# A single-core two-block transformer kernel: reordering its second attention stage and turning the sign of its logits

## What is computed

```
q, k normalised by head (RMS), B heads' last 32 dimensions rotated
logits = (q . k) * scale + bias or causal mask
p      = exp(logits - rowmax(logits));  p = p / rowsum(p)
out    = p . v
x      = x + concat(out_A, out_B) @ w_o
```

## Time and profile before

| what | value |
|---|---|
| median of 3 runs | 827.97 us (826.56 to 829.21) |
| the profiled execution | 827.33 us |
| its span in the trace | 825.5 us |
| PE busy | 813.6 us (99%) |
| DVE, ACT, POOL busy | 584.4, 464.6, 112.1 us |
| the stage of the change | from 565.8 us (`qk(0)`) to 642.5 us (first product of the last feed-forward part) |

### The profile page before, as it was taken

The page is one execution under the profiler, slowest core; times in us unless marked ns, Lnnn a source line. Parts: engine busy times, 40 slices in busy tenths (PEclk is TensorE's granted clock), DMA queues, the critical chain, the costliest instruction groups (busy, mean ns, idle before and its releaser), DMA issues.

```text
span 825.5 us, 15302 instructions
## 1 busy us (share of the span) xinstructions
PE 813.6 (99%) x6672; PEld 739.2 (90%) x6672; DVE 584.4 (71%) x745; ACT 464.6 (56%) x596; POOL 112.1 (14%) x76
## 2 busy tenths in 40 slices
PE   9999999999999999999999999998999999999998
PEld 7999988999999998888888799987888888888886
DVE  6968994985966587666666687688866875566653
ACT  6769775654443674544444574456676654444442
POOL 0102780660000000000000000000661000000000
PEclk9999999999999999999999999999999999999999
DMA  8845453443554655556555655554331555555541
GB/s 312 289 156 167 165 181 103 160 158 137 176 166 145 225 184 192 175 194 203 180 186 196 201 180 183 169 196 153 104 103 52 204 204 192 177 193 204 194 163 52
DMA packets 23827, 143.93 MB, mean 174 GB/s; under 512 B 2722, under 2 KB 4786, under 8 KB 7376
## 3 DMA queue, kind: packets, MB, share of 16 engines
q1 hardware_dynamic: 22576, 139.47, 49.4%
q0 software_dynamic: 1040, 3.43, 1.2%
q10 hardware_dynamic: 144, 0.04, 0.0%
HBM read 141.87 MB, written 1.06 MB: 173 GB/s over the span
## 4 chain that ended last, share of the span: by engine, by line
PE 91%; DVE 4%; ACT 3%; DMA 1%; issue 0%; SPq 0%; POOL 0%
PE ps L1773 11%; PE ps L1774 11%; PE ps L1775 11%; PE ps L2155 7%; PE ps L2148 7%; PE ps L2064 6%; PE ps L2062 6%; PE ps L2063 6%; PE ps L2153 4%; PE ps L2150 4%; PE ps L1839 1%; PE ps L1946 1%; PE ps L1842 1%; PE ps L1845 1%; DVE wlo L1004 1%; PE ps L1799 1%
## 5 line engine op out<-in xcount | busy, mean ns | idle before, releaser
L1004 DVE TENSOR_TENSOR wlo<-raw,whi 128x2048 fp32r<-128x2048 f32 x128 | 292.7, 2288 | 74.2 <-ACT whi L498 73.0
L498 ACT ACTIVATE whi<-raw 128x2048 fp32r<-128x2048 f32 x128 | 243.7, 1906 | 128.7 <-DMA raw<-w 128.5
L1773 PE MATMUL ps<-xx,whi 128*128 128x256 f32 x840 | 242.5, 289 | 0.0
L1774 PE MATMUL ps<-xx,whi 128*128 128x256 f32 x840 | 238.1, 283 | 0.0
L1775 PE MATMUL ps<-xx,wlo 128*128 128x256 f32 x840 | 238.0, 283 | 0.0
L1773 PEld LDWEIGHTS ps<-xx,whi 128*128 128x128 f32 x840 | 161.5, 192 | 1.8 <-issue 0.5
L1774 PEld LDWEIGHTS ps<-xx,whi 128*128 128x128 f32 x840 | 161.6, 192 | 0.2
L1775 PEld LDWEIGHTS ps<-xx,wlo 128*128 128x128 f32 x840 | 161.5, 192 | 0.0
L2062 PE MATMUL ps<-whi,xx 128*128 128x512 f32 x216 | 84.1, 390 | 0.0
L2063 PE MATMUL ps<-whi,xx 128*128 128x512 f32 x216 | 84.1, 389 | 0.0
L2064 PE MATMUL ps<-wlo,xx 128*128 128x512 f32 x216 | 84.0, 389 | 0.0
(11 more groups left out here) (295 smaller groups left out, 1125.0 us busy)
## 6 DMA issues: line engine op xcount, KB each, us to landing
raw<-w SPq DMA_DIRECT2D x128, 1024.0 KB, 4.9
raw<-w SPq DMA_DIRECT2D x8, 256.0 KB, 7.6
x<-xT SPq DMA_DIRECT2D x4, 256.0 KB, 5.5
raw<-w SPq DMA_DIRECT2D x2, 512.0 KB, 8.3
work<-bias_scratch POOLq DMA_DIRECT2D x1, 1024.0 KB, 6.9
out<-x SPq DMA_DIRECT2D x3, 256.0 KB, 2.4
work<-lnr POOLq DMA_DIRECT2D x1, 512.0 KB, 6.9
work<-sgw POOLq DMA_DIRECT2D x1, 512.0 KB, 7.6
```

Source lines behind the costliest of these rows:

```text
L498: A(hi, full, ACT.Copy).then_inc(sem("hi_ready"), 1)
L1004: V.tensor_tensor(lo, full, hi.bitcast(F32), ALU.subtract)\
L1773: mm(out, hi, xh[:, tile, :], start=start, stop=False, skip_group_check=skip)
L1774: mm(out, hi, xl[:, tile, :], start=False, stop=False, skip_group_check=skip)
```

## The change

All of it lies in the second attention stage and just ahead of it.

1. **Sign.** The A keys' gain and the B keys' gain are multiplied by -1, the bias is subtracted instead of added, and the mask is negated once (a new DVE instruction), so that `logits_row` makes minus the logits. Their row minimum is then directly the bias of `exp(-1 * l + min)`; L1479 falls away in all eight steps. `softmax_exp` waits for the two minima (steps 0 to 3) or for the four custom instructions (steps 4 to 7).
2. **PE's order.** The 48 blocks of `w_uq` go in six pieces of eight with a `qk` and `turn`, or a `pv`, between two pieces; `qk(1)` and `turn(0)` come behind the first piece instead of ahead of it. Groups go to banks 0, 1, 2, 0. The first two units of `w_o` are cut in smaller parts that are spread over steps 4 to 6, and the two units overlap. `rope_turned` comes ahead of all of these.
3. **DVE's order.** `rotary` goes ahead of the stage. `logits_row(p)` comes ahead of `queries_factor(p - 3)`; `keys_norm` goes from behind `heads_lo(1)` to behind `logits_row(2)`; the low part of the last `w_uq` unit a step earlier; the two `add_wo` of the first unit behind `logits_row(5)`.
4. **ACT's order.** The two sines go ahead of two squares; `softmax_exp(0)` ahead of `keys_copy(0)`; `rope_copy` and one `split_hi` ahead of `softmax_exp(1)`.

PE's order, as the diff has it:

```diff
-            qk(1)
-            turn(0)
-            for n in range(3):
...
-                for blk in range(16):
...
-                    if blk == 8:
-                        pv(n)
-                        if n == 0:
-                            rope_turned()
-                        if n == 2:
-                            keys_turned(0)
...
-                used(last)
-                if n:
-                    queries_stats(n - 1)
-                qk(2 + n)
-                turn(1 + n)
+            rope_turned()
+
+            def queries(first, end):
...
+                    if i == 0:
+                        pe.wait_ge(sem("evac0"), FILLS[U_UK][0])
+                    elif i % 12 == 0 and j < 3:
+                        pe.wait_ge(sem("uk_ev"), j)
+                    elif i % 12 == 0:
+                        pe.wait_ge(sem("uq_ev"), 1)
+                    last = mm3(ps[j % 3][:, (h % 2) * T:(h % 2 + 1) * T], u % SLOTS, blk * P, k, k == 0, k == 5)
...
+            queries(0, 8)
+            qk(1)
+            turn(0)
+            queries(8, 16)
+            pv(0)
+            queries(16, 24)
+            qk(2)
+            turn(1)
+            queries(24, 32)
+            pv(1)
+            queries(32, 40)
+            qk(3)
+            turn(2)
+            queries_stats(0)
+            queries(40, 48)
+            pv(2)
+            keys_turned(0)
+            pe.wait_ge(sem("uq_ev"), 3)
+            wo_part(0, 0, range(4), (1, 2))
+            wo_part(0, 1, range(4), (1, 2))
+            qk(4)
+            turn(3)
+            queries_stats(1)
+            wo_part(0, 2, range(4), (1, 2))
+            pv(3)
+            keys_turned(1)
+            pe.wait_ge(sem("uq_ev"), 4)
+            wo_part(1, 0, (0, 1), (0, 1))
+            wo_part(1, 1, (0, 1), (0, 1))
+            qk(5)
+            turn(4)
+            queries_stats(2)
+            used(wo_part(0, 3, range(4), (1, 2)))
+            wo_part(1, 2, (0, 1), (0, 1))
+            pv(4)
+            wo_part(1, 3, (0, 1), (0, 1))
+            pe.wait_ge(sem("wo_x"), 1)
+            for k in range(3):
+                wo_part(1, k, (2, 3), (0, 1))
+            used(wo_part(1, 3, (2, 3), (0, 1)))
+            qk(6)
+            turn(5)
+            queries_stats(3)
 
             pe.wait_ge(sem("wo_x"), 2)
-            wo_part(2, 0, (0, 1), (1, 2))
+            wo_part(2, 0, (0, 1), (2, 0))
             pv(5)
```

DVE's and ACT's programs, cut to what moves:

```diff
-                            ins = V.scalar_tensor_tensor(L[:, sl], ps[3 + hh][:, sl], rh[:, r:r + 1], tab[s], ALU.mult, ALU.add)
+                            ins = V.scalar_tensor_tensor(L[:, sl], ps[3 + hh][:, sl], rh[:, r:r + 1], tab[s], ALU.mult, ALU.subtract)
...
-                V.tensor_scalar(smx[:, p % 2, 1, :], smx[:, p % 2, 0, :], -1.0, None, ALU.mult).then_inc(sem("head_max"), 1)
+                    V.tensor_reduce(m4[:, :, 0], L2[:, :, 0:P], AX, ALU.min).then_inc(sem("head_max"), 1)
+                    V.tensor_reduce(m4[:, :, 1], L2[:, :, P:384], AX, ALU.min).then_inc(sem("head_max"), 1)
...
             logits_row(2)
-            ahead(U_UK)
+            keys_norm()
             normalise(2)
             heads_lo(1)
-            keys_norm()
-
+
+            logits_row(3)
             queries_factor(0)
-            logits_row(3)
             ahead(U_UQ)
...
+            logits_row(5)
+            queries_factor(2)
             dve.wait_ge(sem("unit_used"), U_WO + 1)
-            add_wo(0, 0)
-            add_wo(1, 1)
-            queries_factor(2)
-            logits_row(5)
+            add_wo(0, 1)
+            add_wo(1, 2)
             ahead(U_UQ + 2)
             normalise(5)
             heads_lo(4)
             ahead(U_WO)
 
+            logits_row(6)
             queries_factor(3)
-            logits_row(6)
...
+            softmax_exp(0)
             keys_copy(0)
-            softmax_exp(0)
             keys_copy(1)
+            rope_copy()
 
             probs_copy(0)
+            ahead(U_UK)
             softmax_exp(1)
             heads_hi(0)
-            rope_copy()
-            ahead(U_UK)
             queries_evac(0)
```

More of the change, by code:

```diff
@@ L820, in _ @@
             ahead(U_KR)
-            heads_sq(2)
-            ahead(U_KA)
-            heads_sq(3)
             act.wait_ge(sem("ang"), 1)
@@ L827, in _ @@
             A(cosk[64:96, 0, :], ang[64:96, 0, :], ACT.Sin).then_inc(sem("sin"), 1)
+            heads_sq(2)
+            ahead(U_KA)
+            heads_sq(3)
             ahead(U_KA + 1)
@@ L833, in softmax_exp @@
             def softmax_exp(p):
-                act.wait_ge(sem("head_max"), p + 1)
+                if p < 4:
+                    act.wait_ge(sem("head_max"), 2 * p + 2)
+                else:
+                    act.wait_ge(sem("head_l"), 4 * p + 4)
                 for hh in range(2):
@@ L1573, in _, with rotary @@
             V.tensor_scalar(a_, a_, lim, -lim, ALU.min, ALU.max).then_inc(sem("ang"), 1)
+            def rotary():
+                dve.wait_ge(sem("sin"), 2)
+                sgn = cst_s[64:96, C_SIGN:C_SIGN + 1]
+                link(V.tensor_copy(cosq[64:96, 0, :], cosk[64:96, 0, :]))
+                link(V.tensor_scalar(sinq[64:96, 0, :], sink[64:96, 0, :], col("qb_swap", 0, 64, 96), sgn, ALU.mult, ALU.mult))
+                V.tensor_scalar(sink[64:96, 0, :], sink[64:96, 0, :], col("kb_swap", 0, 64, 96), sgn, ALU.mult, ALU.mult).then_inc(sem("rope"), 1)
+                dve.wait_ge(sem("rope"), 1)
+                o_ = krope[64:96, 0, :]
+                link(V.scalar_tensor_tensor(o_, k_, col("kb", 0, 64, 96), cosk[64:96, 0, :], ALU.mult, ALU.mult))
+                link(V.tensor_tensor(s_, s_, sink[64:96, 0, :], ALU.mult))
+                V.tensor_tensor(kr[96:128, 0, :], o_, s_, ALU.add).then_inc(sem("rope"), 1)
             ahead(U_KR)
@@ L1576, in _ @@
             scaled_heads(3)
+            rotary()
             ahead(U_KA)
@@ L1661, in _ @@
             logits_row(1)
-            rotary()
             keys_sums()
+            ahead(U_UK)
             normalise(1)
@@ L1695, in _ @@
             ahead(U_WO)
+            logits_row(6)
             queries_factor(3)
-            logits_row(6)
             dve.wait_ge(sem("unit_used"), U_WO + 2)
-            add_wo(2, 2)
-            add_wo(3, 0)
+            add_wo(2, 0)
+            add_wo(3, 1)
             heads_lo(5)
@@ L1710, in _ @@
             dve.wait_ge(sem("wo_x"), 4)
-            for m, bank in enumerate((1, 2, 0, 3)):
+            for m, bank in enumerate((2, 0, 1, 3)):
                 if m % 2 == 0:
@@ new lines, in _ @@
+            rope_turned()
+            def queries(first, end):
+                for i in range(first, end):
+                    n, blk = divmod(i, 16)
+                    h, k = divmod(i, 6)
+                    j, u = h // 2, U_UQ + n
+                    if blk == 0:
+                        arrived(u)
+                    if i == 0:
+                        pe.wait_ge(sem("act_lo"), before("lo", "c") + 4)
+                    if i == 0:
+                        pe.wait_ge(sem("evac0"), FILLS[U_UK][0])
[4 more added lines that the diff above has]
+                    last = mm3(ps[j % 3][:, (h % 2) * T:(h % 2 + 1) * T], u % SLOTS, blk * P, k, k == 0, k == 5)
+                    if i % 12 == 11 and j < 3:
+                        last.then_inc(sem("uq_mm"), 1)
+                    if blk == 15:
+                        used(last)
@@ L2444, in wo_part @@
                 return last
-            for n in range(2):
-                banks = ((0, 1), (2, 0))[n]
-                if n == 0:
-                    pe.wait_ge(sem("uq_ev"), 3)
-                else:
-                    pe.wait_ge(sem("uq_ev"), 4)
-                    pe.wait_ge(sem("wo_x"), 1)
-                wo_part(n, 0, range(4), banks)
-                if n:
-                    wo_part(n, 1, range(4), banks)
-                pv(3 + n)
-                if n == 0:
-                    keys_turned(1)
-                if n == 0:
-                    wo_part(n, 1, range(4), banks)
-                wo_part(n, 2, range(4), banks)
-                used(wo_part(n, 3, range(4), banks))
-                queries_stats(2 + n)
-                qk(5 + n)
-                turn(4 + n)
+            queries(0, 8)
[41 more added lines that the diff above has]
+            queries_stats(3)
             pe.wait_ge(sem("wo_x"), 2)
-            wo_part(2, 0, (0, 1), (1, 2))
+            wo_part(2, 0, (0, 1), (2, 0))
             pv(5)
@@ L2471, in _ @@
             pe.wait_ge(sem("wo_x"), 3)
[L2472 removed]
+            wo_part(2, 0, (2, 3), (2, 0))
             pe.wait_ge(sem("wo_x"), 4)
[L2474 to L2475 removed]
+            wo_part(3, 0, (0, 1), (1, 3))
+            wo_part(2, 1, range(4), (2, 0))
             pe.wait_ge(sem("head_l"), 32)
[L2477 to L2478 removed]
+            wo_part(3, 0, (2, 3), (1, 3))
+            wo_part(3, 1, (0, 1), (1, 3))
             turn(6)
[L2480 removed]
+            wo_part(3, 1, (2, 3), (1, 3))
             turn(7)
```

68 lines of the change are left out of this document (17 added, 51 removed).

## The result

The changed kernel takes 831.22 us (median of 5 runs, 830.97 to 832.70), beside 827.47 us for the kernel before (5 runs, 826.56 to 829.21). The ratio is 1.0048, with a 95% interval of 1.0032 to 1.0064: slower by some 4 us. The profiled execution took 831.22 us, with a span of 829.4 us and a mean clock of 0.996 (before: 0.998).

The account below looks back on a forecast made before the run. PE, busy 99% of the span, was taken as the bound, so only standstills and low clock counted. Removed -5.95 and added 5.15 + 1.55 + 2.4 + 0.8 + 0.3 gave +4.2 us: 832.0 us median, range 828.5 to 835.0.

Parts of the forecast that it names:

- the wait before `turn(0)`: PE's standstill before turn(0), waiting for normalise(0) on DVE, would go: -2.46 us.
- the low clock behind it: PE's lower clock from turn(0) to the next products with the values would go: -1.55 us.
- the sums of squares: PE's wait for heads_lo(1) on DVE before sums of squares would go: -0.86 us.
- waits for `probs_copy`: PE's waits for ACT before products with the values: 0.86 before pv(3) goes, and 0.22 of the other two.
- wait A: New PE wait before the first w_o product, for the third queries_evac on ACT: +5.15 us.
- the clock at A: PE's clock falls at the standstill before the first w_o product, charged like the old fall: +1.55 us.
- wait B: New PE wait before pv(5), for queries_factor(3) behind step 6's logits on DVE: +2.4 us, between 1.5 and 4.1.
- the clock at B: PE's clock may fall again at the wait before pv(5), 1.55 us at most; half taken, +0.8 us.
- `turn(2)`: At turn(2), normalise(2) on DVE, now behind keys_norm, ends between 0 and 1.28 us late; +0.3 us taken.
- "faster" rival: Before the first w_o product: ACT takes out group 2 within 1.9 us of pv(2)'s start; 824.4 us, chance 0.06.
- The sign: Eight DVE negations of 0.17 us go and one on the mask comes, on no path of PE: 0 us.
- what would show it: Signs expected in the profile after, among them no wait before turn(0) and DVE's busy time down some 2 us.

Follow-up runs that it names:

- the early eviction: Changed kernel with queries_evac(2) moved ahead of softmax_exp(3), behind probs_copy(2), in ACT's list: 824.77 us, 0.9966 of the kernel before.
- both repairs: Changed kernel with queries_evac(2) behind probs_copy(2) on ACT and queries_factor(3) ahead of logits_row(6) on DVE: 822.67 us, 0.9938 of the kernel before.
- the head of the stage put back: Changed kernel with qk(1) and turn(0) again issued ahead of the first piece of eight blocks: 837.06 us, 1.0108 of the kernel before.
- A alone filled: Changed kernel with 22 unused unit-matrix products on PE ahead of its wait for the third queries_evac: 831.74 us, 1.0039 of the kernel before.

## Why the prediction was right

The forecast was 832.0 us for the median, slower with 0.77, with its own bounds of 830.5 to 834 (828.5 to 835.0 with the rivals' nearer parts); measured was 831.22. Against its own execution the sum was +4.2 us, measured +3.9. By its steps:

| step | predicted | in the trace |
|---|---|---|
| the wait before `turn(0)` | -2.46 | -2.46 |
| the low clock behind it | -1.55 | -1.55 |
| the sums of squares | -0.86 | -0.86 |
| waits for `probs_copy` | -1.08 | -1.1 |
| wait A | +5.15 | +5.19 |
| the clock at A | +1.55 | +2.3 to +2.8 |
| wait B | +2.4 | +1.88 |
| the clock at B | +0.8 | 0 in this execution, about 3.1 in another |
| `turn(2)` | +0.3 | +0.17 |
| PE's own work in the new order | 0 | +0.1 to +0.2 |
| sum | +4.2 | +3.7 to +4.3; the stage has +4.18 |

The clock at A is 2.3 us on the 24 products alone, and 7.96 - 5.19 = 2.8 by the stage of the run with the early eviction. PE's own work is the stage less its waits and its low clock: 76.70 - 5.21 - 1.55 = 69.94 us before, and 70.06 and 70.16 in the versions with the early eviction and with both repairs, in which the clock stayed up.

**Some luck is in the total.** The clock at A was put 0.8 to 1.2 us too low; B was put 0.5 too high and the fall at B 0.8 too high for this execution, and these errors cancel.

**The removed part** came off to the tenth. With the head of the stage put back, a wait and its clock returned with 3.07 and 2.5 us; that wait is ended by `rope_copy`, so it is not the same 2.46.

**Wait A** was right to 0.04 us, because its chain starts at `pv(2)` and ACT's list behind that did not move: 7.02 us against the 7.03 from the earlier trace rows. The last 0.3 us of that agreement are luck. Before, `heads_hi(2)` started 1.19 us after `pv(2)`, as ACT came straight from `softmax_exp(3)`; in the change it started after 0.92, and `keys_evac` then waited 0.18 us for PE's transposes. By both ways `keys_evac` started 1.49 us after `pv(2)`. The run with the early eviction showed the "faster" rival's mechanism: had ACT taken out group 2 in time, the kernel would have been faster. It named 824.4 us, and the run gave 824.77; but that sum had left out the 0.8 for the clock at B and the 0.3 for `turn(2)` of the main sum, with which it would have named 825.5. What kept it at a small chance, that ACT's order is written out, was right as well.

**The clock at A** is the term that was mis-sized: 1.55 was the one price that the trace before had. There the clock was low for 3.4 us (573.2 to 576.6, all of it with PE at work), and in the change for 6.8 (600.7 to 607.5), of which PE worked 5.6; all 24 products of `w_o` ran under it, and it cost 2.3 us. It was not the length of the wait that set this: in the run with the head put back the same 5.19 us had 3.4 us of low clock behind them, and a price of 1.25. **The clock at B**, "half a fall, 0.8", was the right kind of guess with the wrong size: it falls in some executions and not in others, and costs 3.1 us where its cost could be read. In the five runs of the change the mean clock is 0.996 four times, which in the profiled one is the fall at A alone, and 0.994 once; that the fifth had a fall at B as well is likely and not shown.

**Wait B** was 1.88, inside the bounds of 1.5 to 4.1 but under the 2.4 that I took. The chain on DVE is 10.24 us against my 10.4, the work of PE 8.5 against 8.9. The 0.9 us that I had added for POOL did not come: of the two low parts one took 2.44 and the other 2.29 us, near the 2.28 of the earlier trace rows. It was POOL that waited, and the trace before had shown as much: there its rotations beside low parts took 3.4 us three times. Its timeline, first before, then in the changed kernel:

```profile
616.32 3.40 POOL L474 TENSOR_TENSOR work<-work 32x512 f32<-32x512 f32 x1
...
620.16 3.33 POOL L474 TENSOR_TENSOR work<-work 32x512 f32<-32x512 f32 x1
```

The rotation took 1.30 us beside no low part (at 597.66), and here 3.33, from just after the start of the low part (619.90) to a moment within the next instructions on DVE. Of these it held one up in turn: the first product of `normalise(5)` took 1.11 us (622.47), where the same shape takes 0.28 elsewhere, and ended with the rotation. The next low part was waiting for its high part then, so this cost nothing; it was so before, too (618.70). The sharing that the Trainium skill states (GPSIMD Engine Reference, Specifications) is thus seen in this trace, but it did not make the low parts late. Taken strictly it gave B = 4.1 and a sum of +5.9 us, which is 2 us off; no sharing gave B = 1.5, the closest to the 1.88, but a sum of +3.3, further from the +3.9 than mine.

**The sign** was costed at nothing, and the two runs of one half each show nothing: 1.0003 for the sign alone, and 0.29 us of the stage for its absence. One sentence of "what would show it" was wrong: DVE's busy time was to fall by 2 us, and fell by 0.2. The negations are gone, but of their 3.0 us 1.7 was above the 0.17 that each takes by itself (1.26 in the one beside POOL's rotation), and such waiting passed to others: two small additions take 2.92 us (585.66; 0.75 before) and the mask's negation 1.34 (596.51).

## What to carry to other kernels

When the work of the busiest engine is put into another order, follow each result that it needs back to the list of the engine that delivers it, and move that step as well: here the new order was worth 5 us as soon as the eviction and the factor came earlier in lists that the change had left alone, and cost 4 without. A wait whose chain starts at an instruction that moves along with it could be computed to 0.1 us from the old trace here; the clock behind it could not, and should be priced as a range (here 1.25 to 3.1 us for one fall). An instruction's time beside POOL is partly waiting, so removing it saves nothing where the next one on the engine then waits in its place.

## What the runs showed of the hardware

- The cost of a fallen clock is not fixed. One fall cost 1.55 us (before, behind 2.46 us of standing still), 2.3 (the change, behind 5.19), 2.5 (behind 3.07), and 3.1 (behind 1.89). In the same kernel the fall behind wait A cost 1.25 us, though the wait was the same 5.19.
- What these five costs follow is the time that PE worked under the low clock: 3.4, 5.6, 5.6, 6.8 and 2.85 us in that order, so between 0.41 and 0.46 us of cost for each us. The low stretches themselves were 3.4 us twice (before, and behind A with the head put back) and 6.8 us three times; which of the two came was not foreseen by the length of the wait.
- The same wait of 1.88 us lets the clock fall in some executions and not in others: with 1.6 us of it filled by needless products, 18 of 18 runs had a mean clock of 0.999 or more; without, 12 of 18 had 0.998 or less (the early eviction and A alone filled). On what it depends was not tried.
- Needless products can thus pay: with the early eviction they brought the median from 824.77 to 823.57 us (0.9966 [0.9952, 0.9981] and 0.9937 [0.9921, 0.9954]) while adding 1.83 us to PE's busy time. Removing the wait (822.67 us, 0.9938) was as good, and needs no such work.
- The shared access of DVE and POOL works both ways, and in these cases the one that started later took longer by about what was left of the other. Beside a POOL rotation that had begun, a DVE instruction of 0.17 us took 1.26 and a low part of 2.28 took 3.32; beside a low part that had begun, a POOL rotation of 1.30 us took 3.33.
